# Modulation products on four column groups of TensorE, in a fused three-layer transformer kernel

## The reference, cut to what matters

```
mod = silu(c) @ w_mod + b_mod
shift1, scale1, gate1, shift2, scale2, gate2 = split(mod, 6)
h = rms_norm(x, g_pre_mix) * (1 + scale1) + shift1
x = x + gate1 * rms_norm(hybrid_mixer(h), g_post_mix)
h = rms_norm(x, g_pre_ffn) * (1 + scale2) + shift2
x = x + gate2 * rms_norm(moe_ffn(h), g_post_ffn)
```

## Time and profile before

| | |
|---|---|
| three runs | 2796.97, 2796.16, 2788.69 us; median 2796.16 |
| the profiled execution | 2793.87 us, span of its instructions 2792.1 us |
| PE busy | 2680.0 us, 96% of the span, 12234 MATMUL records |
| DVE, ACT, GpSimd busy | 2067.6 (74%), 1633.9 (59%), 243.6 us (9%) |
| DMA | 700 MB, mean 251 GB/s |
| mean granted TensorE clock | 0.984 of 2.4 GHz |

### The profile page before, as it was taken

How to read it: one execution, slowest core, us unless ns; L and a number is a source line. 1 busy time by engine, 2 the same in 40 slices (tenths; PEclk the granted TensorE clock), 3 DMA queues, 4 the chain that set the end, 5 groups by cost and what they waited for, 6 DMA issues and landing times.

```text
span 2792.1 us, 38436 instructions
## 1 busy us (share of the span) xinstructions
PE 2680.0 (96%) x12234; PEld 2150.6 (77%) x12234; DVE 2067.6 (74%) x2438; ACT 1633.9 (59%) x2055; POOL 243.6 (9%) x213
## 2 busy tenths in 40 slices
PE   8996999999999999999999999889999899989999
PEld 5654888888888888888878877677788787867787
DVE  4656999999999999999975567765655555877554
ACT  2322888888888888888854434534444344345443
POOL 0001111111111111111100000000000000200000
PEclk9997999999999999999999999999999999999999
DMA  8745999999999999999965654244556456533554
GB/s 312 251 154 195 335 365 362 359 360 358 366 361 360 363 358 359 358 362 361 353 229 188 189 183 161 99 166 147 167 188 220 133 186 207 154 122 129 181 185 146
DMA packets 263482, 700.34 MB, mean 251 GB/s; under 512 B 29512, under 2 KB 128240, under 8 KB 213680
## 3 DMA queue, kind: packets, MB, share of 16 engines
q1 hardware_dynamic: 249780, 685.19, 69.3%
q0 software_dynamic: 9504, 8.42, 0.9%
q10 hardware_dynamic: 4124, 5.77, 0.6%
HBM read 706.57 MB, written 23.63 MB: 262 GB/s over the span
## 4 chain that ended last, share of the span: by engine, by line
PE 84%; DVE 7%; issue 3%; DMA 2%; ACT 2%; SPq 1%; POOL 1%; POOLq 0%; DVEq 0%; ACTq 0%
PE bank L667 22%; PE bank L669 22%; PE bank L668 22%; PE bank L1190 3%; PE bank L1192 3%; PE bank L1191 3%; PE bank L793 1%; DMA raw<-in_w_in 1%; PE bank L817 1%; PE bank L1049 1%; PE bank L1015 1%; PE bank L1075 1%; PE bank L759 1%; PE bank L841 1%; PE bank L741 1%
## 5 line engine op out<-in xcount | busy, mean ns | idle before, releaser
L667 PE MATMUL bank<-w_hi,HTh 128*128 128x512 f32 x2824 | 1126.0, 399 | 16.4 <-DVE HTl L1382 9.5
L669 PE MATMUL bank<-w_hi,HTl 128*128 128x512 f32 x2824 | 1103.4, 391 | 0.0
L668 PE MATMUL bank<-w_lo,HTh 128*128 128x512 f32 x2824 | 1102.9, 391 | 0.0
L1331 DVE TENSOR_TENSOR w_lo<-raw,w_hi 128x1024 fp32r<-128x1024 f32 (+3 forms) x406 | 489.0, 1215 | 338.6 <-ACT w_hi L2308 333.5
L2308 ACT ACTIVATE w_hi<-raw 128x1024 fp32r<-128x1024 f32 (+3 forms) x406 | 426.0, 1056 | 477.8 <-PE bank L669 281.1
L667 PEld LDWEIGHTS bank<-w_hi,HTh 128*128 128x128 f32 x2824 | 533.4, 189 | 137.1 <-DVE HTl L1382 13.9
L669 PEld LDWEIGHTS bank<-w_hi,HTl 128*128 128x128 f32 x2824 | 533.1, 189 | 115.6
L668 PEld LDWEIGHTS bank<-w_lo,HTh 128*128 128x128 f32 x2824 | 534.0, 189 | 102.9
L1979 DVE TENSOR_TENSOR w_lo<-arena,w_hi 128x1024 fp32r<-128x1024 f32 x256 | 316.3, 1235 | 37.9 <-ACT w_hi L2509 21.7
L1979 DVE TENSOR_TENSOR w_lo<-raw,w_hi 128x1024 fp32r<-128x1024 f32 x256 | 298.9, 1219 | 3.6 <-ACT w_hi L2554 3.6
L2509 ACT ACTIVATE w_hi<-raw 128x1024 fp32r<-128x1024 f32 x252 | 267.9, 1063 | 55.6 <-PE bank L669 55.6
(11 more groups left out here) (367 smaller groups left out, 2548.9 us busy)
## 6 DMA issues: line engine op xcount, KB each, us to landing
raw<-in_moe_w SPq DMA_DIRECT2D x128, 1024.0 KB, 6.4
arena<-in_moe_w SPq DMA_DIRECT2D x128, 1024.0 KB, 6.3
H<-in_moe_w SPq DMA_DIRECT2D x64, 1024.0 KB
MIX<-in_moe_w SPq DMA_DIRECT2D x64, 1024.0 KB
raw<-in_ffn_w SPq DMA_DIRECT2D x248, 256.0 KB, 3.0
raw<-in_ffn_w_gu SPq DMA_DIRECT2D x164, 256.0 KB, 3.0
raw<-in_w_in SPq DMA_DIRECT2D x76, 512.0 KB, 4.6
raw<-in_ffn_w_down SPq DMA_DIRECT2D x80, 256.0 KB, 2.8
```

The source lines that it names most:

```text
L667: pe.matmul(acc, xh, wh, start=start, stop=False)
L668: pe.matmul(acc, xh, wl, start=False, stop=False)
L669: return pe.matmul(acc, xl, wh, start=False, stop=stop)
L1331: dve.tensor_tensor(lo_at(n, c), raw_at(n, c), hi_at(n, c).bitcast(F32), ALU.subtract).then_inc(lo_done, 1)
```

## The change

`silu(c)` is spread over 32 columns instead of 128. Product `k` goes to the column group `k % 4` of TensorE, and so to 32 of the 128 PSUM partitions; group `j` accumulates `k` = `j` and `j + 4`. The bank then holds four partial rows, each 32 times. ACT copies it to SBUF (`PARTIAL`, one buffer), and one more float32 product with a 128 x 128 matrix of 1/32 (`SHARE`) sums the partitions and spreads the sum over all 128. DVE's bias add reads the bank of that product.

A half thus costs 8 products of 32 columns, an ACT copy, and a summing product, which waits for the copy (`mod_parted`); the copy of the next half waits for the summing product. In the attention the products are now four in each of steps 0 to 9 (40 in all, five halves), with summing products right after the scores in steps 2, 4, 6, 8 and 10; ACT's copy stands at the end of its steps 1, 3, 5, 7 and 9. After it PE waits for all five halves to be read. GLA has the other three halves (8, 8 and 8 products), with a summing product ahead of the second and third eight; the last summing product stands between the two transposes of `H` ahead of the router. The products before and after `out1` are gone. There are five slots for loads instead of four, three of them in memory that was otherwise empty then. At the start `x` is loaded earlier and the last `first` load goes behind `b_mod0`; DVE squares `x` before it takes `scale1`. The bias adds of DVE move along, one of them from behind `dil_out` to ahead of it.

```diff
-MOD_BANK = [3, 2, 3, 6, 7, 6, 7, 6]
-MOD_SLOTS = 4
+MOD_PARTS = [2, 2, 2, 2, 2, 6, 6, 6]
+MOD_BANK = [3, 3, 3, 3, 3, 7, 7, 7]
+MOD_COLS = 32
+MOD_SLOTS = 5
...
-DIL_FILL = [4, 4, 2, 2, 2, 2, 2, 2, 2, 1, 1]
+DIL_FILL = [4, 4, 4, 4, 4, 4, 4, 4, 4, 4, 0]
+DIL_SUMS = (2, 4, 6, 8, 10)
...
+        with ExitStack() as shared:
+            mod_places = [shared.enter_context(nc.sbuf_tensor("mod_place0", [P, 2, 512], F32))]
...
+        with ExitStack() as shared:
+            mod_places += [shared.enter_context(nc.sbuf_tensor(f"mod_place{i}", [P, 2, 512], F32)) for i in (1, 2)]
...
-        order.extend(("first", j) for j in range(4))
+        order.extend([("first", 0), ("first", 1), ("x", None), ("first", 2), ("first", 3)])
         plan_vec("b_mod1", I["b_mod"][0:1, D:2 * D])
         plan_vec("g_pre_mix", I["g_pre_mix"])
-        order.extend([("first", 4), ("first", 5), ("x", None), ("first", 6), ("tables", None), ("first", 7)])
+        order.extend([("tables", None), ("first", 4), ("first", 5), ("first", 6)])
         plan_vec("b_mod0", I["b_mod"][0:1, 0:D])
+        order.append(("first", 7))
...
-        plan_mods(4, 16)
+        plan_mods(4, 17)
...
-        plan_mods(16, 24)
+        plan_mods(17, 24)
+        plan_vec("b_mod5", I["b_mod"][0:1, 5 * D:6 * D])
+        plan_mods(24, MOD_TILES)
         order.extend(out1_late)
...
-        CS = [sb("c_spread", [P, 4, P])[:, :, :], arena_at(10272, 4, P)]
+        CS = sb("c_spread", [P, KD, MOD_COLS])
+        PARTIAL = arena_at(10272, 512)
+        SHARE = sb("share", [P, P])
...
+            def by_columns(acc, k, rows):
+
+                j = k % 4
+                g = slice(MOD_COLS * j, MOD_COLS * (j + 1))
+                return pe.matmul(acc[g, :], CS[:, k, :], rows, start=(k < 4), stop=(k >= 4), tile_position=(0, MOD_COLS * j))
...
-                    earlier = [i for i in range(b) if MOD_BANK[i] == MOD_BANK[b]]
-                    if k == 0 and earlier:
-                        pe.wait_ge(mod_read, earlier[-1] + 1)
+                    if k == 0:
+                        pe.wait_ge(mod_parted, len(FIRST_HALVES) + b)
                     if m % 2 == 0:
                         pe.wait_ge(mod_landed[t % MOD_SLOTS], 16 * (t // MOD_SLOTS + 1))
-                    mm = pe.matmul(bank[MOD_BANK[b]][:, :], spread_c(k), mod_slot(t)[:, k % 2, :], start=(k == 0), stop=(k == KD - 1))
+                    mm = by_columns(bank[MOD_PARTS[b]], k, mod_slot(t)[:, k % 2, :])
                     if m % 2 == 1:
                         mm.then_inc(mod_used, 1)
...
+            def sum_parts(acc):
+                return pe.matmul(acc, SHARE[:, :], PARTIAL, start=True, stop=True)
+
+            def mod_sum():
+
+                b = mod_sums[0]
+                mod_sums[0] += 1
+                if b:
+                    pe.wait_ge(mod_read, b)
+                pe.wait_ge(mod_parted, len(FIRST_HALVES) + b + 1)
+                sum_parts(bank[MOD_BANK[b]][:, :]).then_inc(mod_summed, 1)
...
+                    if i in sums:
+                        mod_sum()
                     if fill is not None:
                         mods(fill[i])
...
+            pe.wait_ge(E("c_act"), 1)
+
+            def first_sum(n):
+
+                pe.wait_ge(mod_parted, n + 1)
+                sum_parts(next_unit()[:, :]).then_inc(unit_done, 1)
+
+            for n in FIRST_HALVES:
                 for k in range(KD):
                     if k % 4 == 0:
                         pe.wait_ge(E(f"piece_in{2 * n + k // 4}"), 16)
-                    mm = pe.matmul(b[:, :], spread_c(k), FIRST[2 * n + k // 4][:, k % 4, :], start=(k == 0), stop=(k == KD - 1))
-                mm.then_inc(unit_done, 1)
+                    mm = by_columns(bank[4 + n], k, FIRST[2 * n + k // 4][:, k % 4, :])
+                mm.then_inc(mod_used, 1)
+                if n == 0:
+                    pe.wait_ge(E("zeroed"), 1)
+                else:
+                    first_sum(n - 1)
+            first_sum(FIRST_HALVES[-1])
...
+            attend(A_DIL, DIL_FILL, DIL_SUMS)
+            pe.wait_ge(mod_read, len(DIL_SUMS))
...
-            mods(7)
-            pe.wait_ge(mod_read, 3)
+            mods(8)
             pe.wait_ge(E("log_a"), 1)
...
-            mods(5)
+            mod_sum()
+            mods(8)
...
-            mods(4)
+            mod_sum()
+            mods(8)
...
-            mods(8)
             gemm("out1", rows_of=(MIX, "mix1"), tail=())
-            mods(8)
             turn_half(H, "h2", 0)
-            mods(5)
+            mod_sum()
             turn_half(H, "h2", 1)
-            mods(3)
...
-            mark(dve.memset(ZERO[:, :].bitcast(F32), 0.0), "zeroed")
+            mark(dve.memset(SHARE[:, :], 1.0 / MOD_COLS), "zeroed")
+            dve.memset(ZERO[:, :].bitcast(F32), 0.0).then_inc(E("zeroed"), 1)
...
-                dve.wait_ge(mod_used, 4 * b + 4)
+                dve.wait_ge(mod_summed, b + 1)
                 dve.tensor_tensor(MOD[i][:, c], bank[MOD_BANK[b]][:, :], vec(f"b_mod{i}")[:, c], ALU.add).then_inc(mod_read, 1)
...
-                if i in (3, 6):
+                if i in DIL_SUMS:
                     mod_block()
-                if i == 6:
+                if i == 4:
                     gain(gate1, "g_post_mix", 0.0)
 
             attend(A_DIL, in_dil)
             signal("dil_out")
-            mod_block()
...
-            mod_block()
...
-            dve.wait_ge(mod_used, MOD_TILES - 11)
+            dve.wait_ge(mod_used, len(FIRST_HALVES) + MOD_TILES)
...
+            gain(scale2, "g_pre_ffn")
             mod_block()
-            gain(scale2, "g_pre_ffn")
...
             mark(ins, "gates")
-            mod_block()
...
+            act.activation(CS[:, :, :], CCOL.unsqueeze(2).to_broadcast([P, KD, MOD_COLS]), ACT.Silu).then_inc(E("c_act"), 1)
+
+            def first_partial(n):
+
+                act.wait_ge(mod_used, n + 1)
+                if n:
+                    act.wait_ge(unit_done, n)
+                act.activation(PARTIAL, bank[4 + n][:, :], ACT.Copy).then_inc(mod_parted, 1)
+
+            def partial(b):
+
+                act.wait_ge(mod_used, len(FIRST_HALVES) + 4 * b + 4)
+                if b:
+                    act.wait_ge(mod_summed, b)
+                act.activation(PARTIAL, bank[MOD_PARTS[b]][:, :], ACT.Copy).then_inc(mod_parted, 1)
+
+            for n in FIRST_HALVES:
+                first_partial(n)
...
-            attend(A_DIL)
+            attend(A_DIL, lambda i: partial(i // 2) if i in (1, 3, 5, 7, 9) else None)
...
             act.activation(az, az, ACT.Ln, bias=1.0).then_inc(E("z_log"), 1)
+            partial(5)
...
+            partial(6)
             turned_to([(GT[:, 0:4, tt * P:(tt + 1) * P], P, 512) for tt in range(TT)])
+            partial(7)
```

More of the change, by code:

```diff
@@ L314, in build @@
         order.append(("moe_bias", None))
-        plan_vec("b_mod5", I["b_mod"][0:1, 5 * D:6 * D])
-        plan_mods(24, MOD_TILES)
         plan_vec("g_post_ffn", I["g_post_ffn"])
@@ L433, in build @@
         mod_used = sem("mod_used")
+        mod_parted = sem("mod_parted")
+        mod_summed = sem("mod_summed")
         mod_read = sem("mod_read")
@@ L451, in build @@
         E = sem
+        FIRST_HALVES = range(4)
         MOD = [MIX[:, 0, :], MIX[:, 1, :]] + [arena_at(D * i, D) for i in range(4)]
@@ L626, in moe_used @@
             return it * MOE_TILES + MOE_TILES + t + 1
+        MOD_PLACES = [t[:, :, :] for t in mod_places] + [MIX[:, :, 512:1024], arena_at(3 * D, 2, 512)]
         def mod_slot(t):
-            if t < MOD_TILES - 8:
-                proj = [PROJ1[:, tt, 0:1024].rearrange("p (k n) -> p k n", k=2) for tt in range(TT)]
-                return (MIX[:, :, 512:1024], arena_at(3 * D, 2, 512), arena_at(2 * D, 2, 512) if t < 16 else proj[0],
-                        arena_at(D, 2, 512) if t < 12 else proj[1])[t % MOD_SLOTS]
-            return arena_at(MO + 2048 + 1024 * (t % MOD_SLOTS), 2, 512)
+            return MOD_PLACES[t % MOD_SLOTS]
         def hi_at(n, c):
@@ L801, in mix_columns, with attend @@
                 return [MIX[:, tt, base + P * k:base + P * (k + 1)] for k in range(4)]
-            def attend(a, fill=None, blocks=(), each=0, turned_after=None):
+            def attend(a, fill=None, sums=(), blocks=(), each=0, turned_after=None):
                 n = len(a.units)
@@ L880, in attend @@
                     pe.wait_ge(fill_read, TT * filled[0])
-            pe.wait_ge(E("c_act"), 2)
-            for n in range(4):
-                b = next_unit()
+            pe.wait_ge(E("c_act"), 1)
[3 more added lines that the diff above has]
+            for n in FIRST_HALVES:
                 for k in range(KD):
@@ L1016, in turn_rows_in @@
                 mm.then_inc(m_gather, 1)
-            pe.wait_ge(E("zeroed"), 1)
+            pe.wait_ge(E("zeroed"), 2)
             zero_bank(bank[0], True, True)
@@ L1744, in mod_block @@
                     vec_over(f"b_mod{i}")
-            first_mod(1)
-            gain(scale1, "g_pre_mix")
```

(27 more changed lines are left out.)

8 lines of the change are left out of this document (3 added, 5 removed).

## The result

The change made the kernel slower: 2816.61 us, the median of four runs (2812.68 to 2819.36), against 2794.04 of the kernel before beside it. The ratio is 1.0078, with an interval of 1.0067 to 1.009. The forecast was 2805 and slower, within 2791 to 2821. Direction and range held; the loss is more than twice the forecast's, 22.6 us between the medians where the sum said +9.4.

The account below looks back on a forecast made before the run. Bound by loads at the start, PE in the attention, the DVE and ACT chain in GLA; +0.8 +6.4 +0.3 +0.6 +1.3 = +9.4 us on 2793.87 gives 2803.3, forecast 2805 since the median was 2.3 higher; range 2791 to 2821.

Parts of the forecast that it names:

- Four products side by side: On PE, four products in four column groups cost one product, 0.91, plus 0.15 for the change of form: 1.06 us.
- The waits at the sums: In the attention, PE waits for ACT's copy ahead of each of five summing products, together 10.1 us.
- The attention at full clock: PE's work falls to 30.3 us, waits add 10.1: 40.4 us instead of 37.3, +3.1.
- The clock in the attention: Waits 0, 2 and 3 each bring a half-clock stretch, 5.1 us, half taken: +2.6, between 0 and +6.
- GLA, +0.3 us: Gains of 0.65 at `log_a` and 0.7 at the state, against +1.6 for half clock, between 0 and +5.
- DVE's last add ahead of `dil_out`: At the attention's end, DVE's last bias add moves ahead of `dil_out`, for which PE waits: +0.7 us.
- The start: The last load, copy and sum delay DVE's add, so `in1` begins later: +0.8 us, between 0 and +2.4.
- out1 +0.6, router +1.3 us: Without the products there, PE idles longer and runs at half clock at out1 and the router; `h2` transposes gain 0.9.
- The loads, at nothing: Earlier loads with five slots cost nothing; if a load is late, PE waits up to 2 us in all.
- Rival (a): The waits come but the clock holds: +1.9 us, 2798, within the noise; chance 0.29.
- (b): Faster: the attention's sums do not wait, as ACT's copy is done within 2.7 us: -9.0, 2786; chance 0.10.
- (c): The column groups do not run side by side: about +26, 2822, or 2810 with partial overlap; chance 0.11.

Follow-up runs that it names:

- the second profile: The changed kernel itself, nothing altered, run and profiled once more: 2807.65 us.
- the first profile: The changed kernel as first run and profiled, against the kernel before: median 2816.61 us, ratio 1.0078.
- the late waits filled: The changed kernel with unread full-width products ahead of the attention's sums and in the waits of GLA, out1, h2 and the router: 2799.74 us, ratio 1.0012.
- groups of eight: The changed kernel with eight attention products every second step, sums one step later: 2798.8 us, ratio 1.0015; with unread products in the late waits too, 2795.0 us, 0.9996.
- the second profile of the kernel before: The kernel before, nothing altered, run and profiled once more: 2791.89 us.
- the filled versions: The changed kernel with two unread full-width products ahead of each attention sum's wait: 2804.79 us, ratio 1.0046; with later waits filled as well, 2799.74 us, 1.0012.

## Why the prediction was right, and where its size was off

- **Four products side by side, 1.06 us.** Right: the trace has 1.06 us for the eight records at full clock, 0.86 from start to start where they are dense. The Trainium skill, page "TensorE: Matmul & The Clock Gate", section "Why this matters for your kernels", gives 2.38 times for three column groups, and the estimate worked out from it was 1.1 us, 3.2 times for four groups; the trace is a little better, and where it is dense they gain 4.0 times (3.44 to 0.86 us).
- **The waits at the sums, 3, 1.3, 2.8, 2.1 and 0.9 us.** Right where PE runs at full clock: the second profile has 2.88, 1.35, 2.89, 1.98 and 0.87, all released by ACT's copy. In the first profile they are 5.9 us instead of 10.1, because a slow PE arrives later at the same copy. The Trainium skill, page "TensorEngine Tiling (Array Packing)", section "PSUM Bottleneck", says that the copy out of PSUM may bind after the fourfold speed-up; the trace agrees as to who releases, but the copy itself takes 0.58 us. What costs is its place behind DVE's and ACT's work on the unit, and moving it removed the wait.
- **The attention at full clock, 40.4 us.** Right: in the second profile PE is busy 35.9 us, with 10.2 us at half clock; without the 5.1 us that these cost, 30.8 us of work are left where 30.3 was forecast, beside waits of 10.0 us.
- **The clock in the attention, +2.6 us.** This term was the wrong size. The step was "If each brings such a stretch, that is 5.1 us, of which I take half, since PE's slower work partly runs into the next wait". In the second profile the three stretches came, and all of the 5.1 us was lost, for the waits were as long as forecast. In the first there are 30.7 us at half clock, 15.4 us lost, of which 4.2 came back as shorter waits: 11 net, beyond the upper end of 6 that I gave. I had taken three stretches of 3.5 us, one for each long wait. Four of the five profiles of this attention have 23.9 to 30.7 us instead: stretches of 6.8 to 17.1 us, and the one of 17.1 us lies over work that hardly waited. That half clock would last so long was not in the prediction, and why it does is not shown.
- **GLA, +0.3 us.** The gains were there: from the gate product to `log_a`'s product 6.5 us instead of 7.1 (-0.6). The clock's part was the second term of the wrong size: +1.6 was taken, beside a gain of 0.7 at the state, and 5.3 us net were lost between L963 and L1000, so some 6 us by the clock, past the upper end of 5 that I gave; 13.6 us of half clock stand there, where none was. The last sum takes 2.07 us there and its eight products 3.2 us. With the late waits filled the same stretch takes 17.9 us, and with groups of eight as well 14.9 (15.6 before).
- **DVE's last add ahead of `dil_out`, +0.7 us.** Right: 1.2 against 0.6 us.
- **The start, +0.8 us.** Measured +1.2 and +1.0.
- **out1 +0.6, router +1.3 us.** Measured +0.4 and +1.2. I had not followed the routing behind it, which lost 1.1 us: its half clock began at 253.2 before and lasts from 242 to 300 after, but for 3.4 us.
- **The loads, at nothing.** Right for the change itself, where PE waits for no load in the attention. In groups of eight PE waited 1.8 and 2.2 us for them.
- **The sum.** Up to the MoE's start the profiles are 18.1 and 16.3 us longer than before, where +9.4 was forecast; the two clock terms hold nearly all of the difference (in the first profile +11 for +2.6, and 6 for +1.6, less the 4.5 us that its `in1` stretch was shorter). Against the second profile of the kernel before the two are 17.4 and 15.6 us longer. From the MoE's start on the first profile lost 5.3 us more, and the second won 2.5 back. The +3.5 and -3.7 us behind the MoE are scatter, as they belong to one and the same kernel; the +1.2 to +2.1 us within the MoE stand between every pair of profiles. Half clock reaches 5.3 and 5.2 us into it after and 3.7 and 3.2 before, which makes 0.7 to 1.0 us of them; the cause of the others remains open.
- **Rival (a), the waits come but the clock holds,** did not happen by itself, but the filled versions come near it: with the attention's clock at 1.00 the median is 8.1 us above before's beside it, and with the late waits filled too, at a clock still below 1.00 there, 3.0 us, near the +1.9 that I had priced. Rivals (b) and (c) fell with the waits and the 1.06 us. (The 2786 of (b) was 1 us too low by its own sum: 2796 less 9.0 is 2787.)

## What to carry to other kernels

Work taken off an engine that then waits for another engine's copy is not yet won: follow the copy's place in its own engine's queue, and put the product that needs it a whole step later. On TensorE a freed gap also costs through the granted clock, at the gap and for microseconds behind it, so price each gap twice, once for its length and once for what runs at half clock after it. And before a difference of a few us between two profiles is explained, profile the same kernel twice.

## What was unexpected of the hardware

- 9 us of unread products ahead of the waits of the sums made the attention 4.0 to 8.7 us shorter (41.9 us, against 45.9 and 50.6) and the kernel 9 to 12 us faster.
- The granted clock of one and the same code differs between executions: from 10.2 to 30.7 us at half clock in five profiles of the changed kernel's attention (two of that kernel itself, three of variants that change nothing there), 0 and 3.4 us in two of the kernel before.
- Half clock and waits trade with each other: at a mean clock of 0.70 the five waits were 5.9 us, at 0.89 they were 10.0.
- The clock rose to full while PE did nothing but products on 32 of 128 columns, without gaps. And it stayed at half for 17.1 us of the attention in which PE was busy for 16.8.
- Four products in four column groups took 0.86 us from start to start where they are dense, exactly a quarter of the 3.44 us of four full-width ones.
